# Stage 1 head work one step later, bias and value loads merged, one wait of stage 2 moved: an encoder layer on one core

## The chip, the core and the metric

The kernel runs on one core of a Trainium2 chip. The metric is the device time of one execution in microseconds (us), the median of three runs. The core has five engines that run their own instruction streams and meet at semaphores: TensorE (PE; its weight loads are listed as PEld), VectorE (DVE), ScalarE (ACT), GpSimd (POOL) and SyncE (SP), which here issues nearly all transfers (DMA).

## The reference

One encoder layer over a prompt of 512 and a sample of 2048 tokens, 1024 wide, in float32:

```python
x = layer_norm(x, ln_in_g, ln_in_b)
proj = x @ w_in          # GLA q,k,v,gate, low rank; attention q,k,v
o_gla = gla_mixer(...)   # 4 heads, chunks of 64 tokens, forward and backward
o_na = neighbourhood_attention(nq, nk, nv, na_rpb)   # 8 heads, 8x16 windows on rows of 64
mix = concatenate([o_gla, o_na]) @ w_out
x = layer_norm(ALPHA * x + mix, ln1_g, ln1_b)
f = conv_gated_mlp(x, w_up, conv_w, conv_b, w_down)
x = layer_norm(ALPHA * x + f, ln2_g, ln2_b)
```

In `gla_mixer` each head has log decays `la = log_sigmoid(lr @ w_gate + b) / 16`, summed within a chunk, and from them scaled queries and keys, masked scores in a chunk, and a state carried from chunk to chunk. In the attention each score gets a bias `na_rpb[head, row offset, column offset]` ahead of the softmax.

## The kernel before

Every matrix product is done in three passes (high by high, high by low, low by high part) into one accumulator; those matmuls are lines L76 to L78. Both sequences form one row of 2560 tokens, in 5 blocks of 512. There are three stages, each ended by a barrier of all engines.

**Stage 1, `project_gla`**, counts steps n = 0 to 159 of `dense(n)`: four passes over the columns of `w_in` (QK: steps 0 to 39, VG01: 40 to 79, VG23: 80 to 119, NV: 120 to 159), in each 5 blocks of 8 slices of the inner dimension; a step is 12 matmuls. After the eighth step of a block (n % 8 == 7) `evict` moves the four accumulators out. In the VG passes ACT first takes the silu of one half (L555), then DVE copies the other half (L726); in the other passes ACT and DVE copy two accumulators each. The next step's `dense` waits on `copied[u]`. "Boundary 48" below is the point between steps 47 and 48.

The GLA work of a head and block hangs on those steps. `IN_AT[h][b]` is the step of its first part: logits on PE (+0), softplus on ACT (+1), `cumulate` on DVE (L731 to L741, +2), the exponentials on ACT (+3), `scale` on DVE (L748, L750, +4), `turn_keys` on PE (+6), the copy of the turned keys (+7), `chunk_sums` on PE (+8), `copy_sums` on ACT and DVE (L610, L765, +9). `OUT_AT[h][b]` is that of its output: scores on PE (+0), `mask` on DVE (L786, +1), outputs on PE (+2), norm (+3, +4), turning back (+6) and its copies (+7, +8). `updates` (L778, DVE) carry the states on; their steps follow from those of `copy_sums` and `OUT_AT`. Each engine runs its program in step order, and within a step in a fixed order of kinds: on ACT and DVE `evict` comes first, on DVE then `copy_sums`, `scale`, `mask`, `normalise`, `cumulate` and `updates`; on PE `dense` comes first, then logits, turned keys, sums, scores, outputs. So a part that falls on a step with n % 8 == 7 stands behind that step's `evict`, and one at n % 8 == 6 ahead of it.

SP issues each step's loads: xt slices (`load_xt`, 512 KB), 5 steps ahead in stage 1 and 6 in stage 2, and in pass NV also `copy_bias(a)`: a transfer from memory to memory that lays out `rpb_rep`, 16 shifted copies of the bias rows of each head, from which stage 2 reads each query row's own window.

**Stage 2, `natten`**, has 4 pairs of heads, each with 40 dense steps of 6 matmuls, and 20 attention jobs per pair, which begin at step 18 of the pair, one every 2 steps. SP loads everything: `load_xt`, raw weight slices (`load_w`; ACT and DVE split them into high and low parts), `load_bias(p)` and `load_v(p, i)`. POOL adds the masks to the bias (`table`). The first xt and weight loads, `load_bias(0)` and three constants are issued ahead of step 0; the 16 transfers of `load_v(0, i)` at step 3 + i, for i = 0 to 4. PE waits for the constants (`consts_in`: row mask, column mask, identity) ahead of step 0; it needs the identity only in `turn`, where the first job's weights are transposed, at step 23. Each step's `load_xt` stands ahead of that step's other loads.

**Stage 3, `trunk`**, does the output projection, both layer norms and the MLP. 

Of the kernel before, what the change touches and what calls it, by code (L numbers as in the profile page):

```python
# [41 lines left out]
NA_H, DH = 8, 64  # L42
# [38 lines left out]
class Store:  # L81
# [22 lines left out]
    def start(self):  # L104

        with self.nc.Block() as block:
# [7 lines left out]
PER_PASS = NBLK * KC  # L114
# [10 lines left out]
IN_AT = {0: [44, 52, 60, 68, 76], 1: [48, 56, 64, 72, 80], 2: [108, 112, 116, 120, 124], 3: [128, 132, 136, 140, 144]}  # L125
OUT_AT = {0: [95, 98, 101, 104, 107], 1: [111, 115, 119, 123, 127], 2: [143, 147, 151, 154, 157],
          3: [159, 162, 165, 168, 171]}
# [3 lines left out]
def project_gla(nc, x, ln_g, ln_b, w_pass, w_lr, w_gate, b_gate, norm_g, ident_in, causal_in,  # L131
# [53 lines left out]
    with nc.cleanup_on_exit(), ExitStack() as ctx:  # L185
# [121 lines left out]
        def _(sp):  # L307
# [44 lines left out]
            def copy_bias(a):  # L352
                src = rpb_pad[:, ROWS_U - 1 - a:ROWS_U - 1 - a + BIAS_ROWS, :].rearrange("h (o r) x -> h o (r x)", o=1)
                sp.dma_start(rpb_rep[:, a], src.to_broadcast([NA_H, QB_C, BIAS_ROWS * RPB_C])).then_inc(rep_done, 16)
# [81 lines left out]
            for n in range(STEPS):  # L436
# [35 lines left out]
                if NV * PER_PASS <= n < NSTEP and n % 4 == 2 and (n - NV * PER_PASS) // 4 < ROWS_U:  # L472
                    copy_bias((n - NV * PER_PASS) // 4)
            for u in range(UNITS):
                sp.wait_ge(out_stored[u], 16 * stored_by(NPASS * NBLK))
            sp.wait_ge(rep_done, 16 * ROWS_U)
# [586 lines left out]
def natten(nc, xt_s, w_pair, tok_v, rpb_rep, col_mask, row_mask, ident_in, mix_hi, mix_lo):  # L1063
# [17 lines left out]
    with nc.cleanup_on_exit(), ExitStack() as ctx:  # L1081
# [66 lines left out]
        def _(sp):  # L1148
# [10 lines left out]
            def load_bias(p):  # L1159
                need(sp, table_done, 6 * len(PARTS) * p)  # L1160
                for side in range(2):
                    for a in range(ROWS_U):
                        base = rpb_rep[2 * p + side, a]
                        src = bass.AP(tensor=base.tensor, offset=base.offset + QB_C - 1,
                                      ap=[[BIAS_ROWS * RPB_C - 1, QB_C], [RPB_C, BIAS_ROWS], [1, BIAS_COLS]])
                        sp.dma_start(bias[a * QB_C:(a + 1) * QB_C, side], src).then_inc(bias_in, 16)

            def load_v(p, i):
                g0, g1, after = GROUPS_AFTER[i]
                if p:  # L1170
                    sp.wait_ge(pv_done, (p - 1) * JOBS + after)
                by_row = tok_v[:, p * P:(p + 1) * P].rearrange("(g a c) d -> a c g d", a=KG, c=GRID_W)
                for cb in range(NQB):
                    for a in range(KG):
                        sp.dma_start(v[a * BAND:(a + 1) * BAND, g0:g1, cb, :],
                                     by_row[a, BAND_AT[cb]:BAND_AT[cb] + BAND, g0:g1]).then_inc(v_in[i], 16)
# [20 lines left out]
            for n in range(STEPS):  # L1197
                if n + N_AHEAD < NSTEPS:
                    load_xt(n + N_AHEAD)
                for m in range(RAWS, PAIRS * KC):  # L1200
                    if max(split_step(m) - RAWS, 0) == n:
                        load_w(m)
                for i, (_, _, after) in enumerate(GROUPS_AFTER):
                    if n == 3 + i:
                        load_v(0, i)
                    for p in range(1, PAIRS):
                        if n == start[(p - 1) * JOBS + after - 1] + 9:
                            load_v(p, i)
# [10 lines left out]
        def _(pool):  # L1219
            pool.wait_ge(consts_in, 48)  # L1220
            for p in range(PAIRS):
                pool.wait_ge(bias_in, (p + 1) * 2 * 16 * ROWS_U)
# [138 lines left out]
        def _(pe):  # L1361
# [31 lines left out]
            def turn(j):  # L1393
                groups = UNITS_NA[jobs[j][1]][1]
                for side in range(2):
# [6 lines left out]
            def weigh_values(j):  # L1402
# [4 lines left out]
                if cb == 0:  # L1407
                    need(pe, o_lo, unit_no(j))
                    for i, (g0, g1, _) in enumerate(GROUPS_AFTER):
                        if g0 < first + groups and first < g1:  # L1410
                            pe.wait_ge(v_in[i], 16 * NQB * KG * (p + 1))
# [6 lines left out]
            pe.wait_ge(consts_in, 48)  # L1418
# [711 lines left out]
def encoder(nc, a, y_all):  # L2130
# [8 lines left out]
    rpb_rep = scratch("rpb_rep", NA_H, ROWS_U, QB_C, BIAS_ROWS * RPB_C)  # L2139
# [71 lines left out]
```

## Time and profile before

| | us |
|---|---|
| median of three runs | 3434.52 (3432.31 to 3434.90) |
| profiled execution: its own time | 3436.67 |
| profiled execution: span | 3434.9 |
| PE busy in the span | 3188.1 (93%) |
| DVE, ACT, POOL busy | 1761.0, 1123.9, 431.0 |
| stage 1, stage 2, stage 3 (about) | 0 to 811, 811 to 1330, 1330 to 3435 |

The span runs from the first to the last instruction of the profiled execution, and the little beyond it lies outside the instructions. Busy shares are averages over stages with different limits, so the rows further down are taken by stretch: how long PE, the engine that does most of the work, was idle in each, and what it then waited for. The granted clock (PEclk) is the share of TensorE's full rate that the chip gave it: 1.00 is 2.4 GHz and 0.50 is 1.2 GHz.

### The profile page before, as it was taken

What the parts mean: (1) busy time and instruction counts of PE and PEld (TensorE: products, weight loads), DVE (VectorE), ACT (ScalarE), POOL (GpSimd) and SP (SyncE); (2) the same over time, 40 slices, a digit from 0 to 9 for tenths busy, and PEclk for the clock granted to TensorE, in tenths of its full rate; (3) what the DMA queues carried; (4) which work ended last, traced back from release to release, by engine and by line L of the source; (5) the groups of instructions that cost most, each with busy time, mean ns of one, the idle gap of its engine ahead of it and who ended that gap; (6) DMA issues with size and microseconds to landing.
All of it is one profiled execution on the core that took longest, in us unless ns stands there. A gap on an engine that the chain in (4) does not pass through costs nothing.

```text
span 3434.9 us, 42415 instructions
## 1 busy us (share of the span) xinstructions
PE 3188.1 (93%) x15664; PEld 2551.3 (74%) x15664; DVE 1761.0 (51%) x3399; ACT 1123.9 (33%) x2128; POOL 431.0 (13%) x394
## 2 busy tenths in 40 slices
PE   5898999895899997799999999999999999999997
PEld 3676776673577675588888888888888888888885
DVE  6636846752466664555465334253353533534377
ACT  3336436521234433344242222132222321222222
POOL 2312100003234320000002000030000300011000
PEclk9999999996899998899999999999999999999998
DMA  5777878855677755798696656675565755656553
GB/s 197 283 274 256 280 239 287 278 193 168 218 260 248 245 212 220 259 339 291 243 342 250 250 192 210 217 289 195 196 233 196 289 190 195 234 204 236 192 191 120
DMA packets 269421, 807.97 MB, mean 235 GB/s; under 512 B 46242, under 2 KB 112674, under 8 KB 221856
## 3 DMA queue, kind: packets, MB, share of 16 engines
q1 hardware_dynamic: 236320, 608.12, 51.0%
q10 hardware_dynamic: 21312, 155.20, 12.6%
q0 software_dynamic: 11584, 41.95, 3.2%
q8 instruction: 126, 2.06, 0.2%
q14 instruction: 79, 0.65, 0.1%
HBM read 622.04 MB, written 187.24 MB: 236 GB/s over the span
## 4 chain that ended last, share of the span: by engine, by line
PE 58%; DVE 2%; DMA 1%; SPq 0%; ACT 0%; issue 0%; POOL 0%; DVEq 0%
PE trunk_ps_h L76 12%; PE trunk_ps_h L77 12%; PE trunk_ps_h L78 12%; PE trunk_ps_f L76 7%; PE trunk_ps_f L77 7%; PE trunk_ps_f L78 7%; DMA trunk_raw<-in_w_out 1%; PE trunk_ps_h L2051 0%; DVE trunk_y L1812 0%; DVE trunk_stats L1816 0%; DMA trunk_raw<-in_w_up 0%; DVE trunk_w L1793 0%; DVE trunk_y L1849 0%; DVE trunk_y L1851 0%; ACT trunk_w L1710 0%
## 5 line engine op out<-in xcount | busy, mean ns | idle before, releaser
L76 PE MATMUL trunk_ps_h<-trunk_xt,trunk_w 128*128 128x512 f32 x1760 | 685.8, 390 | 1.4 <-DVE trunk_xt L1857 1.4
L77 PE MATMUL trunk_ps_h<-trunk_xt,trunk_w 128*128 128x512 f32 x1760 | 685.6, 390 | 0.0
L78 PE MATMUL trunk_ps_h<-trunk_xt,trunk_w 128*128 128x512 f32 x1760 | 685.6, 390 | 0.0
L1887 DVE SCALAR_TENSOR_TENSOR trunk_tt<-trunk_hb,trunk_cw,trunk_tt 128x512 f32<-128x512 f32 x220 | 187.1, 850 | 678.6 <-ACT trunk_tt L1736 678.6
L76 PE MATMUL trunk_ps_f<-trunk_w,trunk_m 128*128 128x512 f32 x1168 | 457.1, 391 | 20.0 <-DMA trunk_m<-mix_lo 19.2
L78 PE MATMUL trunk_ps_f<-trunk_w,trunk_m 128*128 128x512 f32 x1168 | 455.3, 390 | 0.0
L77 PE MATMUL trunk_ps_f<-trunk_w,trunk_m 128*128 128x512 f32 x1168 | 455.3, 390 | 0.0
L1734 ACT ACTIVATE trunk_hb<-trunk_ps_h 128x512 f32<-128x512 f32 x220 | 131.7, 599 | 886.7 <-PE trunk_ps_h L78 886.7
L76 PEld LDWEIGHTS trunk_ps_h<-trunk_xt,trunk_w 128*128 128x128 f32 x1760 | 331.0, 188 | 70.8 <-DVE trunk_xt L1857 1.8
L77 PEld LDWEIGHTS trunk_ps_h<-trunk_xt,trunk_w 128*128 128x128 f32 x1760 | 330.9, 188 | 68.8
L78 PEld LDWEIGHTS trunk_ps_h<-trunk_xt,trunk_w 128*128 128x128 f32 x1760 | 330.9, 188 | 68.6
L76 PEld LDWEIGHTS trunk_ps_f<-trunk_w,trunk_m 128*128 128x128 f32 x1168 | 219.8, 188 | 66.6 <-issue 19.7
L1746 ACT ACTIVATE trunk_m<-trunk_g 128x512 fp32r<-128x512 f32 x220 | 129.5, 626 | 401.7 <-PE trunk_ps_f L78 365.7
L78 PEld LDWEIGHTS trunk_ps_f<-trunk_w,trunk_m 128*128 128x128 f32 x1168 | 219.7, 188 | 45.9
L77 PEld LDWEIGHTS trunk_ps_f<-trunk_w,trunk_m 128*128 128x128 f32 x1168 | 219.9, 188 | 45.1
L1902 DVE TENSOR_TENSOR trunk_m<-trunk_g,trunk_m 128x512 fp32r<-128x512 f32 x220 | 143.7, 686 | 200.2 <-ACT trunk_m L1746 200.2
L76 PE MATMUL front_acc<-front_w,front_xr 128*128 128x512 f32 x480 | 202.4, 422 | 29.8 <-DVE front_out L726 29.8
L76 PE MATMUL near_acc<-near_xr,near_w 128*128 128x512 f32 x320 | 147.4, 461 | 54.2 <-DMA near_ident<-in_ident 23.9
L78 PE MATMUL front_acc<-front_w,front_xr 128*128 128x512 f32 x480 | 193.5, 403 | 0.0
L77 PE MATMUL front_acc<-front_w,front_xr 128*128 128x512 f32 x480 | 193.3, 403 | 0.0
L1736 ACT ACTIVATE trunk_tt<-trunk_ps_h,trunk_cw 128x512 f32<-128x512 f32 x220 | 170.3, 774 | 0.0
L1897 DVE SCALAR_TENSOR_TENSOR trunk_tt<-trunk_hb,trunk_cw,trunk_tt 128x512 f32<-128x512 f32 x220 | 164.0, 746 | 0.8
(208 smaller groups left out, 4569.7 us busy)
## 6 DMA issues: line engine op xcount, KB each, us to landing
trunk_w<-wu_s SPq DMA_DIRECT2D x88, 1024.0 KB, 4.8
trunk_w<-wu_s ACTq DMA_DIRECT2D x88, 1024.0 KB, 4.8
near_xr<-xt_s SPq DMA_DIRECT2D x160, 512.0 KB, 5.8
front_xr<-xt_s SPq DMA_DIRECT2D x120, 512.0 KB, 5.9
wu_s<-trunk_w SPq DMA_DIRECT2D x44, 1024.0 KB, 4.8
trunk_w<-wd_s SPq DMA_DIRECT2D x44, 1024.0 KB, 4.8
trunk_w<-wd_s ACTq DMA_DIRECT2D x44, 1024.0 KB, 4.8
trunk_raw<-in_w_up SPq DMA_DIRECT2D x44, 512.0 KB, 5.8
```

The costliest lines, as they stand in the source:

```text
L76: pe.matmul(out, lh, rh, start=first, stop=False, skip_group_check=skip)
L77: pe.matmul(out, lh, rl, start=False, stop=False, skip_group_check=skip)
L78: return pe.matmul(out, ll, rh, start=False, stop=last, skip_group_check=skip)
L1734: act.activation(hb[:, i, s, at:at + BLK], ps_h[:, u % NBANK, :], ACT.Copy)
L1736: act.activation(tt[:, i, s, :], ps_h[:, u % NBANK, :], ACT.Identity, bias=tap[:, 3:4], scale=tap[:, at:at + 1]).then_inc(h_out, 1)
L1746: act.activation(m[:, 0, r % NGK, :], g[:, k, :], ACT.Copy).then_inc(gk_hi, 1)
L1887: dve.scalar_tensor_tensor(out, hb[:, i, s, a_j:a_j + BLK], tap[:, a_j:a_j + 1], out, ALU.mult, ALU.add).then_inc(conv_step, 1)
L1897: dve.scalar_tensor_tensor(out, hb[:, i, s, b_j:b_j + BLK], tap[:, b_j:b_j + 1], out, ALU.mult, ALU.add).then_inc(conv_step, 1)
L1902: dve.tensor_tensor(m[:, 1, r % NGK, :], g[:, r % FC, :], m[:, 0, r % NGK, :].bitcast(F32), ALU.subtract).then_inc(gk_lo, 1)
```

## The change

Five edits. All numbers in `IN_AT` and `OUT_AT` grow by one step. `copy_bias` is cut in two (one side of each pair of heads at a time), so that both sides of a pair lie behind each other in `rpb_rep`: 16 transfers of half the size, every 2 steps, in the place of 8 every 4 steps; the bytes are the same. `load_bias` then fetches both sides of a row in one transfer: 8 for a pair and not 16. For pair 0 `load_v` loads all 10 row groups at step 8, in 16 transfers and not 80; later pairs keep their 80. And PE's wait for the constants goes from the start of its stage 2 program to `turn(0)`.

```diff
-IN_AT = {0: [44, 52, 60, 68, 76], 1: [48, 56, 64, 72, 80], 2: [108, 112, 116, 120, 124], 3: [128, 132, 136, 140, 144]}
-OUT_AT = {0: [95, 98, 101, 104, 107], 1: [111, 115, 119, 123, 127], 2: [143, 147, 151, 154, 157],
-          3: [159, 162, 165, 168, 171]}
+IN_AT = {0: [45, 53, 61, 69, 77], 1: [49, 57, 65, 73, 81], 2: [109, 113, 117, 121, 125], 3: [129, 133, 137, 141, 145]}
+OUT_AT = {0: [96, 99, 102, 105, 108], 1: [112, 116, 120, 124, 128], 2: [144, 148, 152, 155, 158],
+          3: [160, 163, 166, 169, 172]}
...
-            def copy_bias(a):
-                src = rpb_pad[:, ROWS_U - 1 - a:ROWS_U - 1 - a + BIAS_ROWS, :].rearrange("h (o r) x -> h o (r x)", o=1)
-                sp.dma_start(rpb_rep[:, a], src.to_broadcast([NA_H, QB_C, BIAS_ROWS * RPB_C])).then_inc(rep_done, 16)
+            def copy_bias(a, side):
+                src = rpb_pad[side::2, ROWS_U - 1 - a:ROWS_U - 1 - a + BIAS_ROWS, :].rearrange("h (o r) x -> h o (r x)", o=1)
+                dst = rpb_rep[:, a, :, side * BIAS_ROWS * RPB_C:(side + 1) * BIAS_ROWS * RPB_C]
+                sp.dma_start(dst, src.to_broadcast([PAIRS, QB_C, BIAS_ROWS * RPB_C])).then_inc(rep_done, 16)
...
-                if NV * PER_PASS <= n < NSTEP and n % 4 == 2 and (n - NV * PER_PASS) // 4 < ROWS_U:
-                    copy_bias((n - NV * PER_PASS) // 4)
+                if NV * PER_PASS <= n < NSTEP and n % 2 == 0 and n % PER_PASS < 4 * ROWS_U:
+                    copy_bias(*divmod(n % PER_PASS // 2, 2))
...
-                for side in range(2):
-                    for a in range(ROWS_U):
-                        base = rpb_rep[2 * p + side, a]
-                        src = bass.AP(tensor=base.tensor, offset=base.offset + QB_C - 1,
-                                      ap=[[BIAS_ROWS * RPB_C - 1, QB_C], [RPB_C, BIAS_ROWS], [1, BIAS_COLS]])
-                        sp.dma_start(bias[a * QB_C:(a + 1) * QB_C, side], src).then_inc(bias_in, 16)
+                for a in range(ROWS_U):
+                    base = rpb_rep[p, a]
+                    src = bass.AP(tensor=base.tensor, offset=base.offset + QB_C - 1,
+                                  ap=[[2 * BIAS_ROWS * RPB_C - 1, QB_C], [RPB_C, 2 * BIAS_ROWS], [1, BIAS_COLS]])
+                    sp.dma_start(bias[a * QB_C:(a + 1) * QB_C].rearrange("p s r x -> p (s r) x"), src).then_inc(bias_in, 16)
...
             def load_v(p, i):
-                g0, g1, after = GROUPS_AFTER[i]
+
+                g0, g1, after = GROUPS_AFTER[i] if p else (0, NKG, 0)
...
+                if n == 8:
+                    load_v(0, 0)
                 for i, (_, _, after) in enumerate(GROUPS_AFTER):
-                    if n == 3 + i:
-                        load_v(0, i)
...
             def turn(j):
                 groups = UNITS_NA[jobs[j][1]][1]
+                if j == 0:
+                    pe.wait_ge(consts_in, 48)
...
-            pe.wait_ge(consts_in, 48)
             for n in range(STEPS):
```

The changed file is one line longer from L355 on, so its L727 is L726 of before.

**VectorE at boundary 72** (the end of the fourth block of pass VG01). `front_out<-front_acc` are the copies of `evict`; L731 to L741 is `cumulate`, L778 the updates, L705 the low part of a weight slice. Before:

```order
218 L731 SCALAR_TENSOR_TENSOR front_z<-front_z,front_e 128x512
219 L733 SCALAR_TENSOR_TENSOR front_e<-front_reset,front_z 64x512
220 L735 SCALAR_TENSOR_TENSOR front_e<-front_reset,front_z 64x512
221 L741 TENSOR_TENSOR front_z<-front_e 64x512 x2
222 L778 SCALAR_TENSOR_TENSOR front_state_a<-front_state_a,front_decay 64x128 x2
223 L726 COPY front_out<-front_acc 128x256 x4
224 L705 TENSOR_TENSOR front_w<-front_raw,front_w 128x512
```

After, where L766 is `copy_sums`:

```order
214 L766 COPY front_state_a<-front_bank 64x4x128 x2
215 L779 SCALAR_TENSOR_TENSOR front_region<-front_region,front_decay 64x128 x2
216 L727 COPY front_out<-front_acc 128x256 x4
217 L706 TENSOR_TENSOR front_w<-front_raw,front_w 128x512
218 L732 SCALAR_TENSOR_TENSOR front_z<-front_z,front_e 128x512
219 L734 SCALAR_TENSOR_TENSOR front_e<-front_reset,front_z 64x512
220 L736 SCALAR_TENSOR_TENSOR front_e<-front_reset,front_z 64x512
221 L742 TENSOR_TENSOR front_z<-front_e 64x512 x2
222 L779 SCALAR_TENSOR_TENSOR front_state_a<-front_state_a,front_decay 64x128 x2
```

The copies of `evict` stood behind `cumulate` and now stand ahead of it.

**VectorE at boundary 120** (the end of pass VG23, where outputs of head 1 run beside the first parts of head 2). L786 is `mask`, L748 and L750 `scale`, L802 the low part of a turned output, L791 and L796 `normalise`. Before:

```order
350 L731 SCALAR_TENSOR_TENSOR front_z<-front_z,front_e 128x512
351 L733 SCALAR_TENSOR_TENSOR front_e<-front_reset,front_z 64x512
352 L735 SCALAR_TENSOR_TENSOR front_e<-front_reset,front_z 64x512
353 L741 TENSOR_TENSOR front_z<-front_e 64x512 x2
354 L778 SCALAR_TENSOR_TENSOR front_state_a<-front_state_a,front_decay 64x128 x2
355 L726 COPY front_out<-front_acc 128x256 x4
356 L802 TENSOR_TENSOR front_region<-front_bank,front_region 128x512
357 L791 RECIPROCAL front_rinv<-front_rinv 128x4
358 L796 SCALAR_TENSOR_TENSOR front_o<-front_bank,front_rinv,front_og 128x128 x4
359 L778 SCALAR_TENSOR_TENSOR front_state_a<-front_state_a,front_decay 64x128 x2
360 L748 TENSOR_TENSOR front_z<-front_k,front_z 128x512
361 L750 SCALAR_TENSOR_TENSOR front_kq<-front_q,front_kq 128x512
```

After:

```order
345 L727 COPY front_out<-front_acc 128x256 x4
346 L732 SCALAR_TENSOR_TENSOR front_z<-front_z,front_e 128x512
347 L734 SCALAR_TENSOR_TENSOR front_e<-front_reset,front_z 64x512
348 L736 SCALAR_TENSOR_TENSOR front_e<-front_reset,front_z 64x512
349 L742 TENSOR_TENSOR front_z<-front_e 64x512 x2
350 L779 SCALAR_TENSOR_TENSOR front_state_a<-front_state_a,front_decay 64x128 x2
351 L803 TENSOR_TENSOR front_region<-front_bank,front_region 128x512
352 L792 RECIPROCAL front_rinv<-front_rinv 128x4
353 L797 SCALAR_TENSOR_TENSOR front_o<-front_bank,front_rinv,front_og 128x128 x4
354 L779 SCALAR_TENSOR_TENSOR front_state_a<-front_state_a,front_decay 64x128 x2
355 L749 TENSOR_TENSOR front_z<-front_k,front_z 128x512
356 L751 SCALAR_TENSOR_TENSOR front_kq<-front_q,front_kq 128x512
```

`cumulate` and the updates went from ahead of the copies to behind them; the scaling of the step (L749, L751), and the mask that comes right behind it, follow behind all of it.

**SP at the start of stage 2.** `near_xr` are xt slices, `near_raw` weight slices, `near_bias`, `near_v` and the three constants the other loads. Before:

```order
451 L1152 DMA near_xr<-xt_s 128x1024 x4
452 L1166 DMA near_bias<-rpb_rep 16x16x48 x16
453 L1194 DMA near_rmask<-in_row_mask 128x48
454 L1195 DMA near_cmask<-in_col_mask 128x96
455 L1196 DMA near_ident<-in_ident 128x128
456 L1152 DMA near_xr<-xt_s 128x1024
457 L1157 DMA near_raw<-in_w_pair 128x256 x4
458 L1152 DMA near_xr<-xt_s 128x1024
459 L1157 DMA near_raw<-in_w_pair 128x256
460 L1152 DMA near_xr<-xt_s 128x1024 x2
461 L1175 DMA near_v<-tok_nv 32x128 x16
462 L1152 DMA near_xr<-xt_s 128x1024
463 L1175 DMA near_v<-tok_nv 32x2x128 x16
464 L1152 DMA near_xr<-xt_s 128x1024
465 L1175 DMA near_v<-tok_nv 32x2x128 x16
```

After:

```order
467 L1158 DMA near_raw<-in_w_pair 128x256
468 L1153 DMA near_xr<-xt_s 128x1024 x4
469 L1166 DMA near_bias<-rpb_rep 16x32x48 x8
470 L1195 DMA near_rmask<-in_row_mask 128x48
471 L1196 DMA near_cmask<-in_col_mask 128x96
472 L1197 DMA near_ident<-in_ident 128x128
473 L1153 DMA near_xr<-xt_s 128x1024
474 L1158 DMA near_raw<-in_w_pair 128x256 x4
475 L1153 DMA near_xr<-xt_s 128x1024
476 L1158 DMA near_raw<-in_w_pair 128x256
477 L1153 DMA near_xr<-xt_s 128x1024 x7
478 L1176 DMA near_v<-tok_nv 32x10x128 x16
479 L1153 DMA near_xr<-xt_s 128x1024 x18
```

The bias is 8 transfers for 16, the xt slices up to number 14 stand ahead of all value loads, and xt slice 15 stands behind the one batch of them.

## Rows read from the trace of the kernel before

**Rows 1.** Windows: length, busy us by engine, granted clock, DMA share, GB/s.
```profile
552.00:748.00 196.00, 178.66 (x1038) 138.29 (x1034) 137.94 (x287) 91.05 (x193) 10.26 (x8) 0.95 0.78 253
...
830.00:892.00 62.00, 36.45 (x103) 25.48 (x104) 12.40 (x14) 6.00 (x15) 42.61 (x48) 0.67 0.55 185
...
636.00:672.00 36.00, 29.30 (x154) 22.50 (x152) 33.10 (x67) 18.71 (x31) 3.49 (x3) 0.88 0.99 310
```

**Rows 2.** Waits over the whole span: total us, times, longest.
```profile
PE front_acc L76 <- DVE front_out L726: 29.8, 8, 5.7
PE near_acc L76 <- DMA near_ident<-in_ident: 23.9, 1, 23.9
PE near_acc L76 <- DMA near_xr<-xt_s: 23.7, 6, 5.6
...
PE front_bank L935 <- DVE front_a_b L786: 10.1, 4, 4.7
```

**Rows 3.** Windows behind boundaries, columns as in Rows 1.
```profile
243.80:247.20 3.40, 3.40 (x8) 2.73 (x9) 3.18 (x5) 1.52 (x5) 1.57 (x1) 0.51 0.66 215
...
373.50:380.40 6.90, 4.65 (x11) 3.76 (x12) 5.74 (x13) 2.10 (x5) 2.40 (x2) 0.51 0.84 309
429.60:433.00 3.40, 3.34 (x15) 2.78 (x16) 3.27 (x8) 0.00 (x0) 0.00 (x0) 1.00 0.98 363
```

**Rows 4.** Timeline round step 48: start, us, engine, line, operation [idle before, releaser].
```profile
237.43 0.69 DVE L731 SCALAR_TENSOR_TENSOR front_z<-front_z,front_e 128x512 f32<-128x512 f32 x1 [19.04 <-ACT front_e L575]
...
243.22 1.42 DVE L726 COPY front_out<-front_acc 128x256 f32<-128x256 f32 x4
...
243.80 0.73 PE L76 MATMUL front_acc<-front_w,front_xr 128*128 128x512 f32 x1 [3.27 <-DVE front_out L726]
```

**Rows 5.** Timeline of TensorE at three later boundaries.
```profile
429.66 0.47 PE L76 MATMUL front_acc<-front_w,front_xr 128*128 128x512 f32 x1 [1.09 <-DVE front_out L726]
...
635.26 0.47 PE L76 MATMUL front_acc<-front_w,front_xr 128*128 128x512 f32 x1 [3.72 <-DVE front_out L726]
...
672.34 0.77 PE L76 MATMUL front_acc<-front_w,front_xr 128*128 128x512 f32 x1 [5.65 <-DVE front_out L726]
```

**Rows 6.** Timeline of ScalarE round step 56.
```profile
262.98 0.97 ACT L610 ACTIVATE front_state_a<-front_bank 64x512 f32<-64x512 f32 x2 [2.70 <-PE front_bank L955]
263.85 0.67 ACT L568 ACTIVATE front_z<-front_bank,front_bg 128x512 f32<-128x512 f32 x1
...
267.81 1.28 ACT L555 ACT_TABLE_LOAD   x1
```

**Rows 7.** Timeline of SP where stage 2 begins, and of TensorE's step 15.
```profile
816.12 10.95 SPq L1166 DMA_DIRECT2D near_bias<-rpb_rep  x16
...
829.02 6.47 SPq L1157 DMA_DIRECT2D near_raw<-in_w_pair  x4
...
847.94 7.47 SPq L1175 DMA_DIRECT2D near_v<-tok_nv  x16
...
879.45 10.45 SPq L1152 DMA_DIRECT2D near_xr<-xt_s  x10
...
886.63 0.79 PE L76 MATMUL near_acc<-near_xr,near_w 128*128 128x512 f32 x1 [0.86 <-DMA near_xr<-xt_s]
```

**Rows 8.** Windows of near steps 40 and 41, and 72 and 73.
```profile
951.88:957.86 5.98, 5.98 (x44) 4.38 (x43) 5.33 (x18) 3.84 (x10) 1.55 (x2) 1.00 1.04 366
1037.83:1050.35 12.52, 9.11 (x44) 6.28 (x43) 10.61 (x28) 7.07 (x20) 7.58 (x9) 0.73 0.82 295
```

**Rows 9.** Timeline of SP and ScalarE before near step 72.
```profile
1024.09 8.72 SPq L1166 DMA_DIRECT2D near_bias<-rpb_rep  x16
...
1038.77 0.31 ACT L1243 ACTIVATE near_w<-near_raw 128x128 fp32r<-128x128 f32 x1 [5.82 <-DMA near_raw<-in_w_pair]
```

**Rows 10.** Transfers of 552 to 748 us: issues, KB each, median us to landing.
```profile
front_xr<-xt_s SPq DMA_DIRECT2D x35, 512.0 KB, 6.4
...
rpb_rep<-in_rpb_pad SPq DMA_DIRECT2D x8, 504.0 KB
```

More of the change, by code:

```diff
@@ L471, in _ @@
                     store_mix(j)
-                if NV * PER_PASS <= n < NSTEP and n % 4 == 2 and (n - NV * PER_PASS) // 4 < ROWS_U:
-                    copy_bias((n - NV * PER_PASS) // 4)
+                if NV * PER_PASS <= n < NSTEP and n % 2 == 0 and n % PER_PASS < 4 * ROWS_U:
+                    copy_bias(*divmod(n % PER_PASS // 2, 2))
             for u in range(UNITS):
                 sp.wait_ge(out_stored[u], 16 * stored_by(NPASS * NBLK))
-            sp.wait_ge(rep_done, 16 * ROWS_U)
+            sp.wait_ge(rep_done, 32 * ROWS_U)
             for i in range(TILES):
@@ L1221, in _ @@
             for p in range(PAIRS):
-                pool.wait_ge(bias_in, (p + 1) * 2 * 16 * ROWS_U)
+                pool.wait_ge(bias_in, (p + 1) * 16 * ROWS_U)
                 for i, (row, e0, n, after) in enumerate(PARTS):
@@ L1409, in weigh_values @@
                     for i, (g0, g1, _) in enumerate(GROUPS_AFTER):
-                        if g0 < first + groups and first < g1:
-                            pe.wait_ge(v_in[i], 16 * NQB * KG * (p + 1))
+                        if p == 0:
+                            pe.wait_ge(v_in[0], 16 * NQB * KG)
+                        elif g0 < first + groups and first < g1:
+                            pe.wait_ge(v_in[i], 16 * NQB * KG * (p + (i == 0)))
                 for g in range(groups):
@@ L2138, in encoder @@
     tok_v, tok_g, tok_nv = (scratch(n, TOK, UNITS * P) for n in ("tok_v", "tok_g", "tok_nv"))
-    rpb_rep = scratch("rpb_rep", NA_H, ROWS_U, QB_C, BIAS_ROWS * RPB_C)
+    rpb_rep = scratch("rpb_rep", PAIRS, ROWS_U, QB_C, 2 * BIAS_ROWS * RPB_C)
     mix_hi, mix_lo = scratch("mix_hi", D, TOK), scratch("mix_lo", D, TOK)
```

## The prediction

> **What bounds the kernel now.** I read the windows by stage first. TensorE (PE) does nearly everything; what can be won or lost is its idle time ahead of a barrier, because stage 3 begins only when the first two stages have ended. In stage 1 the windows show PE busy for nine tenths and more, at a clock of .95 [rows 1]; where stage 2 begins only 36.45 of 62 us, at .67 [rows 1]. Next, the waits of PE by releaser [rows 2]: 29.8 us in eight waits for the copies of `evict`, 23.9 us once for the identity, 23.7 us in six for xt slices, 10.1 us in four logits that wait for `mask`. Then the windows behind the boundaries [rows 3]. After the 3.27 us idle at boundary 48 the granted clock is at its lower level for 3.4 us, after that of boundary 80 for 6.9 us; behind the 1.09 us idle at 429.66 [rows 5] it stays at 1.00. So a long stall is paid twice. Last the timeline round each of those waits, to see what is late.
>
> **Pass VG01 (boundaries 48, 56, 64, 72, 80).** `cumulate` starts at 237.43, the copies of `evict` behind it at 243.22, and PE goes on at 243.80 after 3.27 us idle [rows 4]: the copies stand 5.8 us behind work that nobody needs at once. The printed order at boundary 72 shows that this `cumulate` now follows the copies. Of the 29.8 us, 1.09, 3.72 and 5.65 belong to later boundaries [rows 5]; the five of this pass have 19.3. What is late next is ScalarE. Round step 56 its copy of the sums takes .97 us and its softplus runs from 263.85 to 267.81, then comes a table load of 1.28 [rows 6], and the first silu. Now the softplus starts two dense steps ahead of the boundary and not three. A full-clock step is 12 matmuls at 3.40/15 us [rows 3], 2.72 us, so PE is there 5.4 us after the logits. The copy can be done after 3.96 + 1.28 and some .8 for a silu and a copy (two of the four copies in 1.42 [rows 4]), 6.0: a stall of .6 us, and 1 to 2 where the first softplus loads a table more and where weight slices add work. I take 5 stalls of 1.2, 5.9 us: 13.4 won. The five slow stretches hold some 20.6 us of PE work, those of the first and last row 3.40 and 4.65 [rows 3]; at half rate that is 10.3 lost, and stalls near 1.09 should leave one such stretch, 1.7: 8.6 won. Together **−22**; −13 if the stalls halve only, −28 if they vanish.
>
> That is free only while the late `cumulate` still serves its own chain. Exponentials, `scale` and POOL's work on the keys stand between it and `turn_keys`, four steps after it, 10.9 us. By the busy times of that chain I estimate 4.3 us to spare. Without that cover ten of the twenty items (those with `cumulate` at n % 8 == 7) would make PE wait.
>
> **Rest of stage 1.** Where outputs of one head run beside inputs of the next the same move hurts: after boundaries 112, 120, 128 and 144 the chain is copies, `cumulate`, exponentials, `scale`, `mask`, and the next logits wait for that mask, since scores and logits share a bank (the printed order at 120). I estimate its end at 11 us behind the boundary (1 for copies, 5.8, then 1.4 each for scale and mask and 1.5 of ScalarE) and PE at the logits after 6.9 (two dense steps and the scores), so 4 us of wait. Before, the longest such wait was 4.7 and the three others share 5.4 [rows 2]. So 112 wins some 1.5, 120 and 128 lose 4 and 2. The 3.72 and 5.65 at 136 and 144 [rows 5] don't come back as time: DVE was busy 33.10 of 36 us round them [rows 1], so its backlog goes to the next mask. Outputs that now have their mask behind `evict` (104, and 160 at the tail) lose some 3. The 1.09 at 96 is won. Sum **+7**; it can be +15 if each of the four waits reaches 6, and −10 if DVE keeps up and half the 20 us of waits at copies and masks go.
>
> **Start of stage 2.** Before, SP spends 10.95 us on 16 bias transfers, then issues the constants, and weight slices from 829.02; PE begins after the 23.9 us wait for the identity [rows 2, 7]. PE can now begin at about 817, but for three steps only, since slice 3 of the weights is still to come. Eight bias transfers at between .55 (8.72 us for 16 [rows 9]) and .68 us (10.95 for 16) take about 5 us, so slice 3 is issued 5 us sooner; the transfers ahead of it must still land, and I give step 8 a gain of 3 us. From there on, before, each of five batches of 16 value transfers holds SP for 7.47 us [rows 7], one xt slice gets through between batches, and PE runs one step per 8 us until step 15 at 886.63. In the new order xt slices up to 14 are issued ahead of one batch. Step 8 starts near 842, steps 8 to 14 take 7 × 1.36, and PE is at step 15 at 852. The batch starts near 841 (slice 14 waits for its place in the ring) and ends 7.5 us later, and slice 15 lands some 5.8 us after that, at 854. So step 15 comes 32 us sooner. I take **−31**, since POOL's table work now lies under the first jobs. Bounds: no row shows value transfers of ten row groups. If their issue takes twice as long, slice 15 is 7 us later; if in addition the bias gains nothing, −22. Should slice 15 land as soon as PE is there, −36. The first job needs values and constants only at step 23, 10 us later at least, so that wait costs nothing.
>
> **Bias of pairs 2 and 3.** Before near step 72, 16 bias transfers hold SP from 1024.09 for 8.72 us; a raw weight slice behind them lands so late that ScalarE idles 5.82 us, and its copy of the projection, queued behind, starts late [rows 9]. Near steps 72 and 73 take 12.52 us at a clock of .73, and 40 and 41 5.98 at 1.00 [rows 8]; step 112 repeats it. Eight transfers free SP 4.4 us sooner, nearly the 5.82. Of 2 × 6.5 I take **−10**; −4 if an issue of twice the rows takes longer, −13 if all goes.
>
> **`copy_bias`.** The same bytes in twice the transfers. SP's time for 8 more issues is hidden, since xt is issued five steps (13.6 us) ahead and lands 6.4 us after its issue [rows 10]: 7 us to spare. I cost it at nothing; without that cover it is 16 holds of xt, each .8 us for 252 KB at the 310 GB/s of a full stretch [rows 1], or 3.3 at a quarter of it.
>
> The Trainium skill, DMA: Bandwidth & Descriptors, Rules for kernel authors, says that an outermost dimension below 16 confines a DMA to at most that many engines; by it these copies go from 8 engines to 4. No row here shows engines apart. By that rule pass NV would lose some us at xt slices, which is the fourth rival.
>
> **Sum.** −22 + 7 − 31 − 10 = −56. The profiled execution took 3436.67, 2.15 above the median of the runs shown: 3380.7 by it, **3378** against the median.
>
> **Rivals.**
> 1. *The second half of stage 1 gains too* (0.12): DVE isn't busy enough to keep a backlog, and the waits at 136 and 144 go without others in their place. For: outside that block DVE has slack (137.94 of 196 us [rows 1]). Against: 33.10 of 36. +7 becomes −12: 3359.
> 2. *The head shift moves stalls and wins nothing* (0.14): what leaves the boundaries is found at the logits, at `turn_keys` or behind the silu. For: the 4.7 us wait already there [rows 2]. Against: in pass VG01 no mask exists. −15 becomes 0: 3393.
> 3. *Issue of larger transfers costs more* (0.10): start and bias at their low bounds, −22 and −4. For: bias transfers of one size took .55 and .68. Against: the value batches took the same 7.47 with one, two or three row groups. 3393.
> 4. *Copies crowd their transfer engines* (0.07). The windows show transfer engines busy .78 of pass NV and .99 from 636 to 672 [rows 1]; if the copies use half as many engines, those get twice their share: 16 holds of up to 3.3 us where 7 are to spare, so perhaps 8 us of waits, at 128 to 150. 3386.
> 5. *Slower* (0.04): `turn_keys` at the ten late items. Were nothing to spare, each would wait up to 5.8 us (the `cumulate`) and pay 1.7 in clock: 75 us, less the 56: 3453. It decides from 5.6 us an item on. Against: the 4.3 to spare, and POOL idle.
> 6. *It doesn't do what it says* (0.02): PE held as before by the first weights and by SP; within the bound below.
>
> **How the numbers follow.** My forecast has 0.51. Its own range, with the bounds above taken two at a time, is 3362 to 3396. With rivals 1 to 4 the range is 3352 to 3403; beyond lie rival 5, 6 and mishaps together. 0.2% is 6.9 us, about what a measurement of this kernel tells from no change. Faster by more has the forecast and rivals 1 to 4, 0.94; within it 0.025; slower 0.035.
>
> **What would show it.** Right: PE's wait for L727 in five boundaries near 6 us in all and the clock at 1.00 behind most; `cumulate` behind the copies; step 15 of stage 2 some 32 us closer to the barrier, with a wait for xt of at most a few us there; steps 72 and 112 near 6 us for two; a wait of logits for the mask at 113, 121, 129, 145 of some 4 us each. Wrong: a wait of PE for the turned keys, a wait for `front_xr` in pass NV, value issues above .47 us each, or those mask waits gone.

## The result and the profile after

The changed kernel takes 3412.02 us (median of four runs, 3409.93 to 3417.30) against 3433.41 for the kernel before on the same chip: a ratio of 0.9936, 95% interval 0.9922 to 0.9950. It is faster, as forecast, but by 21 us and not 56: the time lies above the range given. The profiled execution took 3410.41 us (span 3408.6), 26.3 less than that of before; the working below goes by these two traces.

| us | before | after |
|---|---|---|
| last dense step of stage 1 ends | 748.4 | 739.5 |
| first load of stage 2 is issued | 811.3 | 812.8 |
| from there to step 15 of stage 2 | 75.3 | 53.3 |
| from there to step 152 of stage 2 | 459.2 | 432.2 |
| stage 3, first matmul to the end | 2093.0 | 2090.9 |

So all that was won lies in stage 2; stage 1 ends 1.5 us later than before. Waits of TensorE over the whole span (total us, times, longest):

```profile
PE near_acc L76 <- DVE near_w L1296: 21.9, 2, 11.1
...
PE front_bank L936 <- DVE front_a_b L787: 15.3, 5, 5.6
PE front_acc L76 <- DVE front_out L727: 13.3, 6, 5.9
...
PE near_acc L76 <- DMA near_xr<-xt_s: 12.2, 1, 12.2
...
PE front_bank L969 <- DMA front_gains<-kq_s: 6.3, 1, 6.3
PE front_bank L936 <- DMA front_lr<-lr_s: 4.4, 1, 4.4
```

The copies of `evict` fell from 29.8 to 13.3 and the xt slices of stage 2 from 23.7 to 12.2 [rows 2]. But the wait of the logits for the mask grew from 10.1 to 15.3; 21.9 for weight slices stand where the identity was; and two waits for loads in stage 1 appear, 6.3 and 4.4. Where they are, on TensorE's timeline:

```profile
242.35 0.47 PE L76 MATMUL front_acc<-front_w,front_xr 128*128 128x512 f32 x1 [1.90 <-DVE front_out L727]
...
326.69 0.47 PE L76 MATMUL front_acc<-front_w,front_xr 128*128 128x512 f32 x1 [1.15 <-DVE front_out L727]
...
350.32 1.22 PE L936 MATMUL front_bank<-front_lr,front_wg 64*128 64x512 f32 x1 [4.36 <-DMA front_lr<-lr_s]
...
500.38 1.19 PE L936 MATMUL front_bank<-front_lr,front_wg 64*128 64x512 f32 x1 [5.60 <-DVE front_a_b L787]
...
658.38 0.76 PE L76 MATMUL front_acc<-front_w,front_xr 128*128 128x512 f32 x1 [5.86 <-DVE front_out L727]
...
745.74 1.65 PE L969 MATMUL front_bank<-front_gains 64*128 64x128 f32 x12 [6.28 <-DMA front_gains<-kq_s]
```

The stalls at boundaries 48 and 72 are 1.90 and 1.15 us; 56 and 64 have 1.05 and 1.15, so that the first four hold 5.25 where 13.9 stood (19.3 for five, with 5.43 of them at boundary 80). At step 77 (350.32) the logits wait for the low rank load, at 113 (500.38) for the mask, boundary 144 (658.38) still waits 5.86 for the copies, and at 745.74 the first scores behind the dense steps wait for their load (`front_gains`). Windows of the start of stage 2, of its steps 72 and 73 (near steps), and of the tail of stage 1, from its last dense step to the first load of stage 2 (length, busy us of PE, PEld, DVE, ACT and POOL, granted clock, DMA share, GB/s):

```profile
818.50:835.30 16.80, 5.72 (x19) 4.33 (x19) 2.76 (x7) 1.81 (x8) 4.24 (x5) 0.70 0.90 235
842.90:858.70 15.80, 10.87 (x47) 8.35 (x45) 1.37 (x2) 1.20 (x2) 15.80 (x16) 1.00 1.14 271
858.70:883.30 24.60, 17.25 (x78) 13.02 (x79) 5.05 (x16) 6.05 (x13) 15.00 (x21) 0.79 1.06 359
...
1016.27:1026.66 10.39, 6.59 (x44) 4.31 (x42) 10.21 (x22) 5.44 (x16) 7.47 (x9) 1.00 0.76 264
...
739.50:812.80 73.30, 48.04 (x300) 34.61 (x300) 24.05 (x63) 13.69 (x63) 0.00 (x0) 0.71 0.44 151
```

In the stretch where the values are loaded the transfer engines now are full, at 1.14 and then 1.06 (shares are of 16 engines and can pass 1 a little where packets overlap); before, 830 to 892 had .55 [rows 1]. SP's own rows there:

```profile
817.66 9.68 SPq L1166 DMA_DIRECT2D near_bias<-rpb_rep  x8
...
842.87 15.83 SPq L1176 DMA_DIRECT2D near_v<-tok_nv  x16
858.74 26.56 SPq L1153 DMA_DIRECT2D near_xr<-xt_s  x18
```

16 value transfers hold SP for 15.83 us, .99 each on average, and slice 15 is behind them. They are not alike: the first three took .44 to .51 us, the seventh 3.54.

### The profile page after: what moved, and what is told of

Its sections match the earlier page's. It is cut to its first block, busy times and chain, and to the rows that moved or that the text cites. A ratio compares the mean times of both kernels' runs of the same rounds, so it can differ in the third digit from the quotient of the medians.

```text
span 3408.6 us, 42337 instructions
## 1 busy us (share of the span) xinstructions
PE 3179.3 (93%) x15664; PEld 2548.7 (75%) x15664; DVE 1760.5 (52%) x3399; ACT 1122.4 (33%) x2128; POOL 429.1 (13%) x394
## 4 chain that ended last, share of the span: by engine, by line
PE 58%; DVE 2%; DMA 1%; SPq 0%; ACT 0%; issue 0%; POOL 0%; DVEq 0%
PE trunk_ps_h L76 12%; PE trunk_ps_h L78 12%; PE trunk_ps_h L77 12%; PE trunk_ps_f L76 8%; PE trunk_ps_f L78 7%; PE trunk_ps_f L77 7%; DMA trunk_raw<-in_w_out 1%; PE trunk_ps_h L2055 0%; DVE trunk_y L1816 0%; DVE trunk_stats L1820 0%; DMA trunk_raw<-in_w_up 0%; DVE trunk_w L1797 0%; DVE trunk_y L1853 0%; DVE trunk_y L1855 0%; ACT trunk_w L1714 0%
## 5 line engine op out<-in xcount | busy, mean ns | idle before, releaser
L76 PE MATMUL trunk_ps_f<-trunk_w,trunk_m 128*128 128x512 f32 x1168 | 457.1, 391 | 19.9 <-DMA trunk_m<-mix_lo 19.3
L76 PE MATMUL front_acc<-front_w,front_xr 128*128 128x512 f32 x480 | 199.6, 416 | 13.3 <-DVE front_out L727 13.3
L77 PE MATMUL front_acc<-front_w,front_xr 128*128 128x512 f32 x480 | 190.7, 397 | 0.0
L78 PE MATMUL front_acc<-front_w,front_xr 128*128 128x512 f32 x480 | 190.5, 397 | 0.0
L76 PE MATMUL near_acc<-near_xr,near_w 128*128 128x512 f32 x320 | 143.8, 449 | 37.0 <-DVE near_w L1296 21.9
```

What stands on the lines that cost most here:

```text
L76: pe.matmul(out, lh, rh, start=first, stop=False, skip_group_check=skip)
L77: pe.matmul(out, lh, rl, start=False, stop=False, skip_group_check=skip)
L78: return pe.matmul(out, ll, rh, start=False, stop=last, skip_group_check=skip)
```

## The experiments

Theory A: the shift wins in pass VG01 and loses it again in the rest of stage 1; stage 2 wins nearly all by the value batch, and less than forecast because SP is held for longer. Rivals stand with each run. Times are medians; ratios are to the kernel before. Profiles differ by some 4 us in stretches that no edit touched (step 39 began between 214.0 and 218.1 us), and seven kernels with the same program of stage 2 (the changed one, and those that alter stage 1 alone or undo the shift) reached its step 8 31.0 to 36.3 us after the first load, step 15 after 53.1 to 57.0, step 40 after 117.6 to 121.5 and step 152 after 432.0 to 436.7. Smaller differences between two of them carry little.

**The parts.** The shift alone on the kernel before, and the changed kernel without it (`OUT_AT` with `IN_AT` in both):

```diff
-IN_AT = {0: [44, 52, 60, 68, 76], 1: [48, 56, 64, 72, 80], 2: [108, 112, 116, 120, 124], 3: [128, 132, 136, 140, 144]}
+IN_AT = {0: [45, 53, 61, 69, 77], 1: [49, 57, 65, 73, 81], 2: [109, 113, 117, 121, 125], 3: [129, 133, 137, 141, 145]}
...
```

> The kernel before with the new IN_AT and OUT_AT alone; all transfers as before. Theory A (the later head work pays for itself and no more: what pass VG01 wins is lost at step 77, where the low rank load comes late, and where the dense steps end, where the next scores wait for a load that waits for a late normalise): stage 1 ends between 810 and 814 us, against 811.3 before and 812.8 in the changed kernel, and the time is 3430 to 3437. Rival B (the shift wins 15 us as forecast, and the halved bias copies of pass NV made the loads late): stage 1 ends near 797 to 803, time 3419 to 3425.

> The changed kernel with the old IN_AT and OUT_AT: only the bias copies, bias loads, value loads and the moved wait. Theory A: stage 1 ends at 811 as before, stage 2 is some 27 us shorter as in the changed kernel, time 3404 to 3409: faster than the whole change. Rival B (the halved copies cost time in pass NV): stage 1 ends at 818 or later, time 3413 to 3420.

The shift alone: 3436.96 us, ratio 1.0004 (0.9994 to 1.0013), stage 1 ends at 814.0. The transfers alone: 3414.22, ratio 0.9944 (0.9929 to 0.9959), stage 1 ends at 811.6. Theory A holds on the shift: it is worth nothing that can be measured. Rival B falls: with the bias copies as before the same waits are there (step 77 waits 4.5, the first scores 6.3), and with the halved ones and the old steps they are not. Theory A had the second run faster than the whole change (3404 to 3409); it is not, and their intervals overlap.

**The values.** Five batches as before (issued at steps 3 to 7 again), two batches of half the rows, and one of the 16 transfers per step:

```diff
-g0, g1, after = GROUPS_AFTER[i] if p else (0, NKG, 0)
+g0, g1, after = GROUPS_AFTER[i]
...
-g0, g1, after = GROUPS_AFTER[i] if p else (0, NKG, 0)
+g0, g1, after = GROUPS_AFTER[i] if p else ((0, NKG // 2, 0), (NKG // 2, NKG, 0))[i]
...
-if n == 8:
-    load_v(0, 0)
+if 0 <= n - 6 < NQB * KG:
+    load_v(0, 0, n - 6)
```

> The changed kernel with the values of pair 0 as before: five batches of 16 at steps 3 to 7. Theory A (the value batches hold back xt slices one by one, and that is nearly all of what stage 2 won): step 15 comes 17 to 21 us later, time 3429 to 3434. Rival B (the start is bound by transfers in any case and bias and wait won most): 5 to 10 us later, 3417 to 3422.

> The changed kernel with pair 0's values in 32 transfers of 5 row groups (160 rows) and not 16 of 10 (320 rows, .99 us each). Theory A (issue costs by rows beyond a floor near .47 us): about .5 us each, 16 us in all, step 15 of stage 2 where it was, time as the changed kernel within noise. Rival B (each transfer costs .99 whatever its size at this place, because of what is queued): 32 us in all, step 15 some 16 us later, time 3425 to 3430.

> The changed kernel with the 16 value transfers of pair 0 issued one per step at steps 6 to 21 and not all at step 8. Theory A (the 12.2 us wait for xt slice 15 is SP's queue behind the batch): that wait goes, step 24 comes 10 to 14 us sooner, time 3398 to 3403. Rival B (the first jobs then wait for values or the bias table): the wait moves to steps 18 to 26 and the time is 3408 to 3413.

Five batches: 3431.07 us, ratio 0.9992 (0.9982 to 1.0003), 19 us above the changed kernel, and step 15 comes 71.9 us after the first load of stage 2, 18.6 later. SP's timeline in that run:

```profile
846.07 7.48 SPq L1176 DMA_DIRECT2D near_v<-tok_nv  x16
853.60 0.42 SPq L1153 DMA_DIRECT2D near_xr<-xt_s  x1
```

One slice between batches, as before [rows 7]. So the value batch is nearly the whole gain. Two batches: 3415.05, ratio 0.9942; 32 transfers of 160 rows hold SP for 18.71 us, .58 each, and step 15 is where it was. Taken as a mean, that fits a price by rows and is not one by transfer. But the single issues do not have a price by rows. In the changed kernel, then with two batches (ns of one: least, median, most; first and last start):

```profile
L1176 SPq DMA_DIRECT2D near_v<-tok_nv x16: 438/821/3542, 842.9 to 857.8; - x16
...
L1176 SPq DMA_DIRECT2D near_v<-tok_nv x32: 436/437/2026, 848.4 to 866.6; - x32
```

Both start from the same .44 us, and what comes on top are long holds of some transfers; the transfer engines' share is 1.14 in the one batch and .92 in the two. One per step: 3421.55, ratio 0.9961 (0.9946 to 0.9976): no faster than in one batch and rather slower, though the intervals just touch. Step 15 did come 9 us sooner, but by step 40 nothing was left of that (121.6 us after the first load, against 117.6). SP's timeline and two windows of it:

```profile
845.10 0.47 SPq L1178 DMA_DIRECT2D near_v<-tok_nv  x1
...
849.45 0.45 SPq L1178 DMA_DIRECT2D near_v<-tok_nv  x1
...
854.78 2.37 SPq L1178 DMA_DIRECT2D near_v<-tok_nv  x1
...
865.76 2.15 SPq L1178 DMA_DIRECT2D near_v<-tok_nv  x1
...
838.00:852.00 14.00, 12.69 (x43) 9.90 (x44) 9.21 (x12) 2.72 (x9) 14.00 (x14) 0.75 0.83 279
852.00:880.00 28.00, 21.43 (x90) 14.61 (x89) 10.23 (x12) 3.69 (x7) 26.73 (x33) 1.00 1.09 264
```

The same 320-row transfers are issued in .43 to .47 us each until about 852 us, and in .66 to 2.4 from then on, where the transfer engines' share goes from .83 to 1.09. So the price is not one of the rows in a transfer either, as my theory had it: SP is held when the engines behind it are full. The values then landed late, and the first job waited 4.1 us for them (the waits have `near_ps_o` on `near_v`).

**The bias, and the wait.** 16 loads of the bias for each pair in the new layout, and the wait for the constants back at the start:

```diff
-for a in range(ROWS_U):
+for side in range(2):
+    for a in range(ROWS_U):
...
-                if j == 0:
-                    pe.wait_ge(consts_in, 48)
+            pe.wait_ge(consts_in, 48)
             for n in range(STEPS):
```

> The changed kernel with 16 bias loads for each pair (256 rows each) from the new layout, in the place of 8 (512 rows). Theory A (issue by rows): SP spends some 11 us at the start against 9.7 and 8 to 9 us for the later pairs against 6 to 6.5; near steps 72, 73, 112 and 113 are 4 us longer in sum, start 1 us later: 3 to 6 us more than the changed kernel. Rival B (issue by transfer): 8 transfers are worth the 10 us forecast: 10 to 13 us more.

> The changed kernel with the wait for the constants back at the start of TensorE's program of stage 2. Theory A (the steps ahead of slice 3 of the weights fill time that is lost anyway, and slice 3 is there some 5 us after the constants): TensorE begins 17 to 18 us after the first load of stage 2, step 8 comes 2 to 5 us later than in the changed kernel, step 15 at most 2, time within noise (3410 to 3416). Rival B (the moved wait is worth the 12 us by which the first step came sooner): 3422 to 3426.

Sixteen: 3417.87 us, ratio 0.9949 (0.9934 to 0.9964); SP spends 11.67 at the start against 9.68 and 8.3 to 8.6 for pairs 1 and 2 against 6.6 to 7.0; stage 2 to step 152 takes 439.5 us against 432.2. That 7.3, of which 2.7 are there by step 40, lies between the two forecasts, nearer to A. Against the 432.0 to 436.7 of the kernels with eight loads it is 3 to 7, which is A's range and not B's. The wait at the start: 3414.87, ratio 0.9937 (0.9922 to 0.9952); TensorE starts 19.8 us after the first load and not 5.7, and at step 8 it is 2.2 us behind the changed kernel, at step 15 1.1. Both lie inside what kernels with the moved wait differ by (31.0 to 36.3 and 53.1 to 57.0), and so does the time: the moved wait is worth nothing that can be told here, as theory A says, since the steps ahead of weight slice 3 fill time that is lost anyway.

**Stage 1.** The low rank load earlier; the last outputs back; then the shift for fewer heads.

```diff
-                for i in at(shifted(in_step, -3), n):
+                for i in at(shifted(in_step, -6), n):
                     load_lr(i)
...
-OUT_AT = {0: [96, 99, 102, 105, 108], 1: [112, 116, 120, 124, 128], 2: [144, 148, 152, 155, 158],
-          3: [160, 163, 166, 169, 172]}
+OUT_AT = {0: [96, 99, 102, 105, 108], 1: [112, 116, 120, 124, 128], 2: [144, 148, 152, 154, 157],
+          3: [159, 162, 165, 168, 171]}
```

> The changed kernel with the low rank load of each item 6 steps ahead of its logits and not 3. Theory A (SP issued it late, held by a weight slice whose place is freed by a split that stands behind the late cumulate): the 4.4 us idle at step 77 goes, and with it the slow clock behind it, 7 to 8 us in all; stage 1 ends at 804 to 807, time 3403 to 3406. Rival D (what is freed there is lost again at the next late thing): the idle goes, stage 1 still ends at 811 to 813, time 3409 to 3413.

> The changed kernel with the last two outputs of head 2 and all of head 3 back at their old steps (154, 157, 159, 162, ...). Theory A: the normalise whose end releases the load of the first scores behind the dense steps stands ahead of the last evict again; the 6.3 us idle of TensorE there falls under 1 us, stage 1 ends 8 to 10 us sooner (803 to 805), time 3402 to 3405. Rival C (that load is late because the transfer engines are full): the idle stays above 4 us and the time is 3409 to 3413.

Low rank load earlier: 3414.78 us, ratio 0.9949. The wait at 77 went, and nothing came of it: rival D in kind, though stage 1 ended at 819.1 and not at 811 to 813, in a profiled execution 6 us above the median. ScalarE's and TensorE's timelines there:

```profile
352.71 0.63 ACT L535 ACTIVATE front_w<-front_raw 128x512 fp32r<-128x512 f32 x1 [1.90 <-DMA front_raw<-in_w_pass]
...
360.45 0.76 PE L76 MATMUL front_acc<-front_w,front_xr 128*128 128x512 f32 x1 [4.92 <-DVE front_out L727]
```

ScalarE waits for a weight slice, its copy of the sums and the softplus come behind that, the silu after them, and boundary 80 has a stall of 4.92 us which the changed kernel does not have. Last outputs back: 3418.03, ratio 0.9952; the wait of the first scores fell from 6.3 to 2.26 us, but stage 1 ended at 816.4. The window of that run's tail:

```profile
744.50:816.40 71.90, 47.42 (x300) 34.10 (x300) 22.04 (x56) 13.66 (x63) 0.00 (x0) 0.75 0.45 153
```

PE is busy 47.42 of 71.90 us, so idle 24.5; in the changed kernel's tail 48.04 of 73.30, idle 25.3. The wait was spread over others, and the dense steps ended 5.0 us later (744.5). Neither theory A nor its rival is right there: the wait goes and the time stays.

The three `IN_AT` of the runs that follow, each in the changed kernel with the old `OUT_AT`:

```diff
+IN_AT = {0: [45, 53, 61, 69, 77], 1: [49, 57, 65, 73, 81], 2: [108, 112, 116, 120, 124], 3: [128, 132, 136, 140, 144]}
+IN_AT = {0: [45, 53, 61, 69, 76], 1: [49, 57, 65, 73, 80], 2: [108, 112, 116, 120, 124], 3: [128, 132, 136, 140, 144]}
+IN_AT = {0: [45, 53, 61, 69, 77], 1: [49, 57, 65, 73, 81], 2: [109, 113, 117, 121, 125], 3: [129, 133, 137, 141, 145]}
```

> The changed kernel with the shift of IN_AT for heads 0 and 1 alone; heads 2 and 3 and all outputs at their old steps. Theory A (the shift wins 16 us in pass VG01, and what loses them again is the later masks behind the copies in passes VG23 and NV, and the late normalise ahead of the tail): the 16 us stay, the dense steps of stage 1 end at 726 to 732 us against 739.5, time 3395 to 3402. Rival B (whatever is won early is lost in the passes that follow, since DVE and SP are late there anyway): the dense steps end at 736 to 741 and the time is 3408 to 3414.

> As the kernel with IN_AT of heads 0 and 1 shifted alone, but the fifth block of both at its old step (76, 80): the low rank load that TensorE waits 5.1 us for at step 77, and the 2.7 us at boundary 96, are then as before. Theory A (the five boundaries are separate, boundary 80 loses its 5.4 us stall again and the other two come back to what they were): within 4 us of that kernel, 3399 to 3406. Rival B (the late load at step 77 costs its whole 8 us): 3393 to 3397.

> The changed kernel with IN_AT shifted for all heads and OUT_AT at its old steps. Theory A (what loses time after pass VG01 are the outputs: their masks now stand behind the copies of evict, and one step more of them is left for the tail): the tail is 63 to 68 us as in the kernels with the old OUT_AT, the stalls at 136 and 144 shrink, time 3394 to 3402. Rival B (the inputs of heads 2 and 3: cumulate behind the copies makes scale and mask late): the dense steps win nothing beyond pass VG01, waits of the logits for the mask are 15 us or more as in the changed kernel, time 3403 to 3411.

First heads only: 3402.99 us, ratio 0.9906 (0.9891 to 0.9921). This beats both kernels: against the changed one it is 9 us faster, and the two intervals just don't overlap. From step 104 to the end of the dense steps nothing of its lead is lost (9.2 us at 104, 9.5 at 159, in a run that was 3.6 us late at step 39, ahead of the shift). The dense steps ended at 738.9 all the same, in rival B's range, and the time lies between the two forecasts. Stage 2 begins 8.5 us sooner than in the changed kernel, and 7.9 of them lie in the tail:

```profile
738.90:804.30 65.40, 45.44 (x300) 32.79 (x300) 19.97 (x50) 13.17 (x62) 0.00 (x0) 0.74 0.47 160
```

65.40 us, PE idle 20.0. First four blocks: 3405.30, ratio 0.9907, the same, as theory A had it; boundary 80 waits 6.99 us there and boundary 96 1.07. Counted from step 39, step 84 comes 6.3 us later than with all five blocks, but the end of the dense steps only 1.0. So the move of the fifth block is worth next to nothing by then: it trades the stall at 80 for the late load at 77 and the longer wait at 96. Inputs only: 3432.93, ratio 0.9992 (0.9980 to 1.0005), slower than both forecasts: the dense steps end at 756.5. New waits of TensorE between 470 and 750 us:

```profile
PE front_bank L984 <- DVE front_state_a L766: 9.0, 4, 2.8
...
PE front_bank L984 <- DVE front_region L766: 5.6, 3, 2.4
```

L984 are the outputs, L766 is `copy_sums`: with inputs one step later and outputs where they were, the two meet, and 14.6 us are lost there beside a clock of .88 in 552 to 748. In the later passes inputs and outputs have to move together, and together they lose 7.5 us.

## Why the prediction was wrong

**Start of stage 2** (forecast −31, measured −22.0 at step 15 and −23.3 at step 24). Step 8 came 3.0 us sooner, which is the number worked out, but that agreement is luck: the shift alone, with the transfers of before, had 2.3 of it. The step that failed is that the batch "starts near 841" and "ends 7.5 us later": it started at 842.87 and ended 15.83 us later. The prediction had named the sign, value issues above .47 us. I took the .47 us of a value transfer in the old batches as its price. It was what SP needs while the transfer engines have room; the merged batch fills them. Rival 3 had the number (−22) with the wrong mechanism: not the size of a transfer costs, but what is queued, as the transfers spread over steps showed. That step 15 then waits for slice 15 is as forecast, with 12.2 us and not "a few".

**Bias of pairs 2 and 3** (−10, measured −3.9). The term was mis-sized: 12.52 and 12.33 us for steps 72, 73 and 112, 113 became 10.39 and 10.50. SP was free only 1.7 us sooner for pair 2 (7.02 against 8.72), not 4.4; half as many transfers cost more than half. Even the 3.9 is one pair of profiles: the four steps took 20.5 to 24.0 us in seven kernels with eight loads, and 24.8, 25.4 and 23.4 in three with sixteen, so some 3. The loads of pair 2 one by one and the window of each, in the changed kernel, then before:

```profile
L1166 SPq DMA_DIRECT2D near_bias<-rpb_rep x8: 430/586/2454, 1002.5 to 1008.6; - x8
1002.50:1009.54 7.04, 7.04 (x47) 5.21 (x45) 4.32 (x16) 2.46 (x8) 0.00 (x0) 1.00 0.96 180
...
L1166 SPq DMA_DIRECT2D near_bias<-rpb_rep x16: 430/448/1372, 1024.1 to 1032.4; - x16
1024.09:1032.80 8.71, 8.71 (x62) 6.45 (x61) 5.72 (x20) 4.05 (x12) 0.00 (x0) 1.00 0.66 155
```

The first issues again take the same (.43 to .49 us for 512 rows, .43 to .45 for 256), and the holds come on top where the share is .96 and not .66. So this term seems to have failed for the reason of the first; that is read from the traces, and no run tests it by itself.

**Pass VG01** (−22, measured −16.5 at step 91). The step on the boundaries held: 5.25 us in the first four (5.9 forecast for five), the clock at 1.00 throughout, and the gain was 18.3 at step 77. What I left out is the work queued behind the late `cumulate` on both engines. The timelines round step 72, where L742 is the end of `cumulate`, L585 the exponentials, L706 a weight slice's low part, L321 the next raw slice, and the last row the low rank load:

```profile
332.27 1.41 DVE L742 TENSOR_TENSOR front_z<-front_e 64x512 f32<-64x512 f32 x2
...
333.71 0.63 ACT L585 ACTIVATE front_z<-front_z 128x512 f32<-128x512 f32 x1 [3.97 <-DVE front_z L742]
...
334.36 0.68 DVE L706 TENSOR_TENSOR front_w<-front_raw,front_w 128x512 fp32r<-128x512 f32 x1
...
335.06 0.33 SPq L321 DMA_DIRECT2D front_raw<-in_w_pass  x1
...
344.74 0.45 SPq L370 DMA_DIRECT2D front_lr<-lr_s  x1
```

ScalarE waits 3.97 us for `cumulate`; the splits of weight slices wait on both engines; SP waits for a place for the next raw slice until 335.06, and all its loads behind that are late. The low rank load for step 77 is issued at 344.74, lands 5.6 us later, and TensorE is idle 4.36 us and at a granted clock of .50 behind it (351.5 to 355.4): 8.1 of the 18.3 lost, of which boundary 80, now without its old stall, gave 6.4 back by step 84. I had looked for what waits at `turn_keys`; it does not wait (rival 5 fell), and SP's queue does.

**Rest of stage 1** (+7 with the tail; measured +7.5 to the end of the dense steps, and +10.4 more for the tail). The first is as forecast in sum, less so in place: the logits wait 5.6, 3.5, 2.7 and 1.7 us at 113, 121, 129 and 145, and boundary 144 still waits 5.86, which I had put behind the next mask; the first of those four was 4.7 before and was to shrink, and the 1.09 at boundary 96, forecast as won, became 2.16. Of the tail I had some 2. From the windows, the tail of the changed kernel is 73.3 us with PE busy 48.0; before it was 62.9 with 43.0 in the same 300 matmuls, at a clock of .78 against .71. So 5.4 are idle time and 5.0 the clock. The idle part has the size of the 6.28 us wait: the load of the first scores waits in SP's program for the normalise of an output two before (L797), which moved to step 159 and stands there behind the last `evict` (L727):

```profile
738.82 0.69 DVE L727 COPY front_out<-front_acc 128x512 f32<-128x512 f32 x1 [0.67 <-PE front_acc L78]
...
740.97 1.13 DVE L797 SCALAR_TENSOR_TENSOR front_o<-front_bank,front_rinv,front_og 128x128 f32<-128x128 f32 x4
...
742.15 0.33 SPq L409 DMA_DIRECT2D front_gains<-kq_s  x1
```

That the wait comes from the new steps is shown (it is in the shift alone and in none of the kernels with the old `OUT_AT` above 3.4), and so is the idle part: PE is idle 24.2 to 25.7 us in the tails of the eight kernels with all the new steps, and 19.6 to 20.0 in those of the four in which heads 2 and 3 and the outputs have the old ones. That this one wait lengthens the tail is not shown, since without most of it the tail stayed at 71.9. How much of the clock's part belongs to the shift stays open too: the tail of those eight has PE busy 46.8 to 53.8 us at granted clocks of .74 to .63, that of those four 43.0 to 47.9 at .78 to .73.

**`copy_bias`** (0, and rival 4). It held: between steps 120 and 159 the shift with the old copies loses 5.4 us to the kernel before, and with the halved ones 5.3; the halved ones without the shift lose nothing to it. One halved copy held SP for 5.47 us in the changed kernel (.79 at most in the shift alone), and no time shows it. By the Trainium skill, DMA: Bandwidth & Descriptors, Rules for kernel authors, the halved copies run on four engines at most; no run here shows engines apart, and no cost.

**The sum.** −16.5 + 7.5 + 10.4 in stage 1 and −25.6 in stage 2 give −24.2; stage 3, which nothing touched, took 2.1 us less in this execution: −26.3. Rivals 2 (0.14) and 3 (0.10) came true together, and the range had held them only one at a time. Slips in the prediction's own sums change nothing of this: five stalls of 1.2 make 6.0 and not 5.9, the items of "Rest of stage 1" add up to some 6.4 and not 7, the early bound of the start is 35 and not 36 by its figures, and its own range, with two bounds at a time, begins at 3355 and not 3362.

## What to carry to other kernels

A transfer's issue time read where the transfer engines are half idle is a floor; before merging transfers or issuing them closer together, add up what must land by the next use and read the DMA share that this would need. When work moves past a fixed point of each block, list on every engine what stands behind it there, down to loads that wait for a buffer's place, and move only those items whose boundary waits: the first heads alone gave 9 us more than all, most of it in the tail. Rivals that act in different stages can both come true, so the range has to add them.

## What the runs showed of the hardware

The same 320-row, 160 KB transfer was issued by SP in .43 to .47 us while the transfer engines had a share of .83, in .99 on average in one batch at 1.14, and in .66 to 2.4 between xt slices at 1.09. And a stretch of the same 300 matmuls with short waits between them, the tail of stage 1, had PE busy 43.0 to 53.8 us in the executions of the different kernels, at granted clocks of .78 to .63.
